# A pass without a step ahead of TensorE's loop over expert steps

## The reference

```python
def hier_moe(h, w_group, b_group, w_router, b_router, w_gate, w_up, w_down):
    ...
    combine = jnp.sum(jax.nn.one_hot(expert, N_EXPERTS, dtype=jnp.float32) * weight[..., None], axis=-2)
    a = jnp.einsum('btd,edf->btef', h, w_gate)
    u = jnp.einsum('btd,edf->btef', h, w_up)
    z = jax.nn.silu(a) * u * combine[..., None].astype(a.dtype)
    return jnp.einsum('btef,efd->btd', z, w_down).astype(h.dtype)
```

## Time and profile before

| | us |
|---|---|
| median of 3 runs | 622.52 (622.03 to 624.54) |
| the profiled execution | 623.2 |
| its span | 621.4 |
| TensorE busy with matmuls | 492.7 (79%) |
| VectorE, ScalarE, GpSimd busy | 225.2, 156.7, 114.5 |
| HBM read | 162 MB |

### The profile page before, as it was taken

One profiled execution on the slowest core, in us unless ns is written; L12 is line 12 of the kernel. 1 busy time (PEld: TensorE's weight loads), 2 busy tenths in 40 slices (PEclk: granted clock), 3 DMA queues, 4 the chain that ended last, 5 costly groups with the idle time before them and its releaser, 6 DMA issues.

```text
span 621.4 us, 8713 instructions
## 1 busy us (share of the span) xinstructions
PE 492.7 (79%) x2920; PEld 264.1 (43%) x2921; DVE 225.2 (36%) x572; ACT 156.7 (25%) x339; POOL 114.5 (18%) x175
## 2 busy tenths in 40 slices
PE   1869999999987999984345776448887988788994
PEld 0448787788633344432331332113433344333442
DVE  0342543142686259899670111010111021111144
ACT  1211434532756203222001111010122121111233
POOL 5030002000084440011010121120222222222200
PEclk9969999999999799988557799688999899999998
DMA  8994864420492951215999599999999898999822
GB/s 276 399 349 184 283 239 162 177 73 0 186 373 57 410 129 68 88 50 218 366 420 330 220 414 420 419 421 419 420 400 408 348 419 320 410 416 362 306 89 85
DMA packets 48544, 172.99 MB, mean 278 GB/s; under 512 B 14776, under 2 KB 24048, under 8 KB 33134
## 3 DMA queue, kind: packets, MB, share of 16 engines
q1 hardware_dynamic: 39034, 150.74, 62.2%
q0 software_dynamic: 9136, 21.76, 9.6%
q10 hardware_dynamic: 340, 0.09, 0.1%
HBM read 162.07 MB, written 27.71 MB: 305 GB/s over the span
## 4 chain that ended last, share of the span: by engine, by line
PE 61%; DMA 17%; DVE 11%; issue 6%; ACT 2%; SPq 2%; POOL 0%; POOLq 0%; DVEq 0%; ACTq 0%
PE PB L1658 17%; PE PB L1933 15%; DMA wB<-in_w_up 9%; PE PB L1958 7%; PE PB L1828 6%; DMA ada_m<-in_w_ada 4%; PE PB L1595 2%; PE PB L1982 2%; DMA ada<-in_w_ada 2%; PE PB L1727 1%; PE PB L1797 1%; PE PB L1912 1%; PE PB L1756 1%; PE PB L1670 1%; PE PB L1980 1%
## 5 line engine op out<-in xcount | busy, mean ns | idle before, releaser
L1933 PE MATMUL PB<-wA,XT 128*32 128x512 f32 x480 | 115.0, 633 | 43.8 <-DMA wB<-in_w_up 23.8
L1933 PE MATMUL PB<-wB,XT 128*32 128x512 f32 x480 | 114.9, 634 | 0.0
L1658 PE MATMUL PB<-hT,win 128*128 128x256 f32 (+1 forms) x448 | 103.9, 392 | 2.0 <-DVE hT L1066 2.0
L1658 PEld LDWEIGHTS PB<-hT,win 128*128 128x128 f32 x448 | 86.0, 194 | 22.5 <-issue 9.4
L1933 PEld LDWEIGHTS PB<-wA,XT 128*32 128x32 f32 x480 | 37.3, 116 | 115.0 <-issue 110.4
L1958 PE MATMUL PB<-wA,zT 128*32 128x512 f32 x240 | 55.8, 606 | 5.7 <-ACT zT L946 5.7
L1504 DVE SCALAR_TENSOR_TENSOR z<-silu_g,w_now,PB 128x256 f32<-128x256 f32 x15 | 7.2, 481 | 145.8 <-ACT silu_g L944 145.8
L1958 PE MATMUL PB<-wB,zT 128*32 128x512 f32 x240 | 55.8, 608 | 0.0
L1828 PE MATMUL PB<-wout,yT 128*128 128x512 f32 x112 | 48.8, 593 | 0.0
L944 ACT ACTIVATE silu_g<-PB 128x256 f32<-128x256 f32 x15 | 5.7, 383 | 135.1 <-PE PB L1933 135.1
L1510 DVE TENSOR_TENSOR yo<-PB,gate_row 128x512 f32<-128x512 f32 x15 | 10.4, 692 | 70.7 <-PE PB L1958 65.7
(11 more groups left out here) (427 smaller groups left out, 686.0 us busy)
## 6 DMA issues: line engine op xcount, KB each, us to landing
wB<-in_w_gate SPq DMA_DIRECT2D x24, 1024.0 KB, 15.5
wB<-in_w_up SPq DMA_DIRECT2D x24, 1024.0 KB, 19.6
wB<-in_w_down SPq DMA_DIRECT2D x24, 1024.0 KB
ada<-in_w_ada POOLq DMA_DIRECT2D x12, 1024.0 KB, 7.5
ada<-in_w_ada SPq DMA_DIRECT2D x8, 1024.0 KB, 11.9
wA<-in_w_gate SPq DMA_DIRECT2D x8, 1024.0 KB, 15.4
wA<-in_w_up SPq DMA_DIRECT2D x8, 1024.0 KB, 18.6
wA<-in_w_down SPq DMA_DIRECT2D x8, 1024.0 KB
```

Of the source, the lines that this page charges most:

```text
L1658: last = pe.matmul(B[(q % 2) * 2 + h][:, 0:cn], win[:, n % 3, k, col:col + P], hT[:, k, c0:c0 + cn], start=(k == 0), stop=(k == KD - 1))
L1933: last = pe.matmul(B[2][32 * g:32 * g + 32, :], XT[:, k, 32 * g:32 * g + 32], gu[:, :, k, :], start=(k == 0), stop=(k == KD - 1))
```

## The change

TensorE's loop counts passes m instead of steps n. Pass 0 has no step: its arm number is 4, which no arm matches, and a third value of the parity table, now called kind, leads to a new branch at the end of the pass, in which the first transposes and the wait for the end of planning stand. Pass m from 1 on does step m - 1. Whether there is another pass is no longer a comparison with nsteps, which isn't known when pass 0 runs, but a table go_i of zeros and ones, read with a register load at each of the three loop levels; nsteps is loaded behind the loop. The tables of TensorE get an entry for pass 0 and are moved up by one; the semaphores that TensorE waits for in a pass (XT_v, XT_a, z_ready, zT_ready by 1, y_v and y_a by 2) are raised ahead of the loop by the engines that own them, so that pass 0 would find them met and later ones wait as before. Loops of the other engines stay as they are.

```diff
-            def one(n):
-                arm = pe.value_load(arm_i[0:1, bass.ds(n, 1)], min_val=0, max_val=ABUF * BBUF - 1)
+            def one(m):
+                arm = pe.value_load(arm_i[0:1, bass.ds(m, 1)], min_val=0, max_val=ABUF * BBUF)
...
-                            pe.wait_ge(XT_v, n + 1)
-                            pe.wait_ge(XT_a, n + 1)
+                            pe.wait_ge(XT_v, m + 1)
+                            pe.wait_ge(XT_a, m + 1)
...
-                parity = pe.value_load(odd[0:1, :, :].rearrange("p a b -> p (a b)")[:, bass.ds(n, 1)], min_val=0, max_val=1)
+                kind = pe.value_load(odd[0:1, :, :].rearrange("p a b -> p (a b)")[:, bass.ds(m, 1)], min_val=0, max_val=2)
                 for p in range(2):
-                    with pe.If(parity == 1 - p):
-                        pe.wait_ge(X_in[p], 8 * n + (24 if p == 0 else 16))
+                    with pe.If(kind == 1 - p):
+                        pe.wait_ge(X_in[p], 8 * m + (16 if p == 0 else 8))
...
-            pe.wait_ge(steps_ready, 1)
-            pe.wait_ge(X_in[0], 16)
-            transpose_X(0, 0)
-            transpose_X(0, 1)
+                with pe.If(kind == 2):
+                    pe.wait_ge(X_in[0], 16)
+                    transpose_X(0, 0)
+                    transpose_X(0, 1)
+                    pe.wait_ge(steps_ready, 1)
+
+            def go(m):
+                return pe.value_load(go_i[0:1, bass.ds(m, 1)], min_val=0, max_val=1)
+
+            with pe.Fori(0, MAXSTEP // 16 + 1) as o:
+                more = go(16 * o)
+                with pe.If(more == 1):
+                    with pe.Fori(0, 4) as i:
+                        more = go(16 * o + 4 * i)
+                        with pe.If(more == 1):
+                            with pe.Fori(0, 4) as j:
+                                more = go(16 * o + 4 * i + j)
+                                with pe.If(more == 1):
+                                    one(16 * o + 4 * i + j)
             nsteps = pe.value_load(steps_i[0:1, 0:1], min_val=MINSTEP, max_val=MAXSTEP)
-            with pe.Fori(0, (MAXSTEP + 15) // 16) as o:
-                with pe.If(nsteps > 16 * o):
-                    with pe.Fori(0, 4) as i:
-                        with pe.If(nsteps > 16 * o + 4 * i):
-                            with pe.Fori(0, 4) as j:
-                                with pe.If(nsteps > 16 * o + 4 * i + j):
-                                    one(16 * o + 4 * i + j)
```

On the other engines (VectorE; ScalarE does the same for y_a, XT_a and zT_ready; GpSimd writes the table odd with a 2 in its first place):

```diff
+            step(dve.memset(arm_i[:, 0:1], ABUF * BBUF))
+            step(dve.memset(wneed[:, :, 0:1], 64))
+            step(dve.memset(go_i[:, 0:1], 1))
             link(dve.memset(LG[:, TT, :], 0.0))
             dve.wait_ge(lg_ps, 1)
...
-            step(dve.tensor_scalar(wneed[:, 0, :], round_i[:, 0, :], 32.0, 32.0, ALU.mult, ALU.add))
+            step(dve.tensor_scalar(wneed[:, 0, 1:NSTEP], round_i[:, 0, 0:NSTEP - 1], 32.0, 32.0, ALU.mult, ALU.add))
...
+            settle()
             step(dve.tensor_copy(steps_i[:, :], steps_f[:, :]))
+            step(dve.tensor_scalar(go_i[:, 1:NSTEP], sgrid[:, 0:NSTEP - 1], steps_f[:, 0:1], None, ALU.is_lt))
...
-            dve.memset(st1[:, 3:4], 0.0).then_inc(y_v, 1)
+            dve.memset(st1[:, 3:4], 0.0).then_inc(y_v, 3)
+            dve.memset(mv[:, 0:1], 0.0).then_inc(XT_v, 1)
+            dve.memset(mv[:, 1:2], 0.0).then_inc(z_ready, 1)
```

More of the change, by code:

```diff
@@ L280, in build @@
         steps_i = late("steps_i", [P, 1], I32)
+        go_i = late("go_i", [P, NSTEP], I32)
         steps_f = late("steps_f", [P, 1])
@@ L601, in _ @@
                                     pattern=[[-P, 2], [32, NS]], channel_multiplier=-1))
-            step(pool.iota(odd[:, :, :], pattern=[[0, (NSTEP + 1) // 2], [1, 2]], base=0, channel_multiplier=0))
+            link(pool.iota(odd[:, :, :], pattern=[[0, (NSTEP + 1) // 2], [-1, 2]], base=1, channel_multiplier=0))
+            step(pool.memset(odd[:, 0, 0:1], 2))
             step(pool.iota(code_a[:, :], pattern=[[ABUF, (LATER_A + ABUF - 1) // ABUF], [33, ABUF]], base=ABUF, channel_multiplier=0))
@@ L707, in scatter @@
             def scatter(s):
-                outputs = counted(2 * s + 3)
+                outputs = counted(2 * s + 5)
                 pool.wait_ge(y_v, outputs)
@@ L932, in _ @@
             act.activation(col[:, 5, :], col[:, 4, :], ACT.Exp).then_inc(top_exp, 1)
-            act.activation(st1[:, 1:2], st1[:, 0:1], ACT.Copy).then_inc(y_a, 1)
+            act.activation(st1[:, 1:2], st1[:, 0:1], ACT.Copy).then_inc(y_a, 3)
+            act.activation(bn[:, 0, 0:1], st1[:, 0:1], ACT.Copy).then_inc(XT_a, 1)
+            act.activation(bn[:, 1, 0:1], st1[:, 0:1], ACT.Copy).then_inc(zT_ready, 1)
             act.wait_ge(idx_made, 2)
@@ L951, in one @@
                 act.activation(ysam[:, 512:D], B[6][:, :], ACT.Copy).then_inc(y_a, 1)
-                act.wait_ge(y_v, 2 * n + 2)
+                act.wait_ge(y_v, 2 * n + 4)
                 act.activation(ysam[:, 0:512], B[5][:, :], ACT.Copy).then_inc(y_a, 1)
@@ L1478, in _ @@
             link(dve.tensor_scalar(place_i[:, :, :], unit_i[:, :, :], 1, None, ALU.bitwise_and))
-            step(dve.scalar_tensor_tensor(out=arm_i[:, :], in0=place_i[:, 0, :], scalar=float(BBUF), in1=place_i[:, 1, :],
+            step(dve.scalar_tensor_tensor(out=arm_i[:, 1:NSTEP], in0=place_i[:, 0, 0:NSTEP - 1], scalar=float(BBUF), in1=place_i[:, 1, 0:NSTEP - 1],
                                           op0=ALU.mult, op1=ALU.add))
-            step(dve.tensor_scalar(wneed[:, 0, :], round_i[:, 0, :], 32.0, 32.0, ALU.mult, ALU.add))
-            step(dve.tensor_scalar(wneed[:, 1, :], round_i[:, 1, :], 64.0, 64.0, ALU.mult, ALU.add))
+            step(dve.tensor_scalar(wneed[:, 0, 1:NSTEP], round_i[:, 0, 0:NSTEP - 1], 32.0, 32.0, ALU.mult, ALU.add))
+            step(dve.tensor_scalar(wneed[:, 1, 1:NSTEP], round_i[:, 1, 0:NSTEP - 1], 64.0, 64.0, ALU.mult, ALU.add))
+            settle()
             step(dve.tensor_copy(steps_i[:, :], steps_f[:, :]))
+            step(dve.tensor_scalar(go_i[:, 1:NSTEP], sgrid[:, 0:NSTEP - 1], steps_f[:, 0:1], None, ALU.is_lt))
             step(dve.tensor_scalar(ends_i[:, 1, 0:1], steps_f[:, :], 4.0, None, ALU.mult))
@@ L1510, in one @@
                 dve.tensor_tensor(yo[:, 0:512], B[5][:, :], gate_row[:, 0:512], ALU.mult).then_inc(y_v, 1)
-                dve.wait_ge(y_a, 2 * n + 2)
+                dve.wait_ge(y_a, 2 * n + 4)
                 dve.tensor_tensor(yo[:, 512:D], B[6][:, :], gate_row[:, 512:D], ALU.mult).then_inc(y_v, 1)
@@ L1917, in lanes @@
                 return [wA[a], wA[a], wB[b][:, 0, :], wB[b][:, 1, :]]
-            def one(n):
-                arm = pe.value_load(arm_i[0:1, bass.ds(n, 1)], min_val=0, max_val=ABUF * BBUF - 1)
-                need_a = pe.value_load(wneed[0:1, 0, bass.ds(n, 1)], min_val=32, max_val=16 * NA + 16)
-                need_b = pe.value_load(wneed[0:1, 1, bass.ds(n, 1)], min_val=64, max_val=32 * NB)
+            def one(m):
+                arm = pe.value_load(arm_i[0:1, bass.ds(m, 1)], min_val=0, max_val=ABUF * BBUF)
+                need_a = pe.value_load(wneed[0:1, 0, bass.ds(m, 1)], min_val=32, max_val=16 * NA + 16)
+                need_b = pe.value_load(wneed[0:1, 1, bass.ds(m, 1)], min_val=64, max_val=32 * NB)
                 for a in range(ABUF):
@@ L1935, in one @@
                             last.then_inc(gu_ps, 1)
[L1936 removed]
+                kind = pe.value_load(odd[0:1, :, :].rearrange("p a b -> p (a b)")[:, bass.ds(m, 1)], min_val=0, max_val=2)
                 for p in range(2):
[L1938 to L1939 removed]
+                    with pe.If(kind == 1 - p):
+                        pe.wait_ge(X_in[p], 8 * m + (16 if p == 0 else 8))
                         transpose_X(p, 0)
[L1941 removed]
+                        pe.wait_ge(z_ready, m + 1)
                         for k in range(2):
@@ L1948, in one @@
                         with pe.If(arm == BBUF * a + b):
-                            pe.wait_ge(zT_ready, n + 1)
-                            pe.wait_ge(y_v, 2 * n + 1)
-                            pe.wait_ge(y_a, 2 * n + 1)
+                            pe.wait_ge(zT_ready, m + 1)
+                            pe.wait_ge(y_v, 2 * m + 1)
+                            pe.wait_ge(y_a, 2 * m + 1)
                             pe.wait_ge(dA_in[a], need_a)
@@ L1990, in _ @@
             add_up(0)
-            pe.wait_ge(y_v, 2 * nsteps + 1)
-            pe.wait_ge(y_a, 2 * nsteps + 1)
+            pe.wait_ge(y_v, 2 * nsteps + 3)
+            pe.wait_ge(y_a, 2 * nsteps + 3)
             add_last(0)
```

## The result

The changed kernel takes 646.76 us in the median (646.57 to 646.79, 4 runs) against 622.46 us (622.03 to 624.54, 4 runs): a ratio of 1.038, 95% interval 1.036 to 1.041. It is slower, by 24.3 us. The prediction said 640 us, 628 to 650.

What follows compares the result with a forecast made beforehand. Bound by step 0's jump into absent code, weight waits in steps 2 to 5, then TensorE and its sequencer alone; 623.2 - 0.7 + 9.5 + 2.7 + 6.8 = 641.5, 640.8 against the median, written 640 us, range 628 to 650.

Steps and rivals of the forecast that it cites:

- The removed stall: Step 0, between gate/up and down matmuls: 6.47 us of issue vanish, down matmuls go from 4.93 to 3.64; together 7.8 us.
- The pass: Ahead of step 0: the pass without a step stalls 6 and 3.5 us on absent code; first matmul 6.2 us late.
- The turns: Between steps: go load 0.65 plus branch 0.26, 0.91 us a turn; 9.5 us for the turns into steps 5 to 13.
- The faster rival: In the turns: added load and branch hide under matmuls already handed over, turn not lengthened; 614.2 or 620.9 us, chance 0.09.
- The way out: From the turn into step 14 to the final sums: added loads and branches, less work removed, cost 2.7 us.
- The front's gain: Up to the turn into step 1: 0.7 us gained in all, bounds 7.4 gained to 3.9 lost.
- The clock: Gate/up matmuls after longer turns start at the lower clock, 1.7 us each; 6.8 us, between 0 and 15.
- hidden in full: Rival: the whole pass fits into the wait ahead of step 0, clock falls no more often; 627.3 us, chance 0.08.

Runs made afterwards that it cites:

- The go load alone: Kernel before the change, with a register load from table go at its three loop levels and no pass without a step: 639.2 us, ratio 1.027.
- the branch alone: Kernel before the change, with a never-taken branch over eight transposes added at each pass's end: 627.5 us, ratio 1.0056.
- the filled turns: Changed kernel with eleven unused 128x128 matmuls placed between the register loads of each turn: 635.96 us, ratio 1.021.
- go covered: Changed kernel with the next pass's go loaded into a register behind the gate/up matmuls, the loop levels comparing that register: 628.26 us, ratio 1.0065.
- the last pair: Next step's arm and need loads put between gate/up matmuls: kernel before 621.97 us; changed kernel, go load behind gate/up and first-pass constants, 615.67 us.

## Why the prediction was right, step by step

- **The removed stall** was right: 6.47 us of issue are gone, the down matmuls are back at 3.64, no branch is long after the pass, and the code stays. From first gate/up to last down matmul step 0 takes 15.23 us in place of 22.40: 7.2 against 7.8 forecast, since its gate/up matmuls took 9.29 instead of 8.60, which the forecast left out.
- **The pass** was right in its mechanism, and within 0.8 us in these: stalls of 5.7 and 4.3 us (6 and 3.5 forecast), transposes at 330.84 (331.5), first gate/up matmul at 335.17 (335.6), step 0's end 1.4 us early (1.6). That the last agree so well is in part luck. The pass began 1.1 us before its forecast (the first go load at 312.1, not 313.2), mostly for the 0.9 us by which the placement products came sooner; without these step 0 would end 0.5 early. The start of the first product lies between 304.49 and 306.37 in the twelve profiles, and does not go by the edits, so a time of the front from one profile is good to a microsecond or so.
- **The turns** were right: ten turns cost 10.9 us more, against 9.5 for nine and 0.91 for the tenth. They did not grow evenly: those into steps 7 and 11 by 2.4 us each, those into steps 8 and 12 by 0.2 each, the others by 0.7 to 1.1, because the loop level of four turns now ends a step earlier. They became 2.0 to 3.9 us, as forecast. The go load alone and the branch alone bear out both parts. The faster rival, a load that lies under matmuls already handed over, is what happens only once the load is moved there.
- **The way out**: 2.7 forecast, 2.4 measured (1.5 at the sums, 0.9 in the turn into step 14).
- **The front's gain** was put at 0.7 after the turn into step 1; 1.7 reached step 4, of which up to 0.9 may be the earlier products just named.
- **The clock** is the term that was mis-sized. "I take half, five, less the one there is: 4 x 1.7 = 6.8": eight fell, not five, one of them by 2.9 us, and the term is 12.9. With it the sum would be 646.9; the other terms are off by 1.0 at most and nearly cancel. The mechanism, idle time ahead of the phase, is borne out by the filled turns. The count is not: it was taken from two turns of the earlier trace rows, of which the longer one (2.79 us) was the one without a fall. A piece of 2.02 us (503.05) was followed by a phase at full clock and one of 2.03 (572.27) by a low one, so the piece's length alone does not decide. What else does is open.

What the prediction did not see is how near the pass was to paying. It counted the pass's own loads as part of the pass, and "hidden in full" as out of reach at 8.8 us without stalls. The loads can be taken out: with constants for the first pass and loads behind matmuls elsewhere, the same pass gains some 6 us.

The theory that the pass gives nothing net held for the kernel with go covered, and fell with the last pair. It had drawn from one comparison in which the turns, and with them the clock, also differed: in the two profiles, three more low phases stand against what the pass gained in front.

## What to carry to other kernels

What a register load costs here depended on its place: ask how many matmuls are queued at that point, and put it between them, not behind the last. In a loop whose turn leaves the engine idle, add the clock to the price of each longer turn, here 12.9 us against 10.9 for the turns themselves, and check it by filling the idle time with matmuls of no use. Code that must come in was paid for once here, by a jump or in sequence; a pass without work helps only so far as it starts inside a wait, so keep its own loads out of its way.

## What the runs showed of the hardware that was not expected

- Eleven matmuls of no use in each turn made the changed kernel 10.8 us faster: the gate/up phases of steps 5 to 14 went from up to 10.05 us to 7.1 at a granted clock of 1.00.
- With the arms in reverse order no branch exceeds 350 ns, and TensorE still stands 3.00 us inside the arm that step 0 takes, behind its second matmul, while q8 moves its packets.
- Three register loads with their checks, moved to a place where the queue was empty, made the down matmuls 5.34 us long instead of 3.64, at a granted clock of 0.68.
